# Matmul shapes and order in a hybrid attention step: prompt's values in four column tiles, new keys' scores over the whole array, sample's values in one stretch

## The chip, the cores and the metric

## What is computed

One layer of a decoder step, for a fresh prompt of 512 tokens and for 8 sequences with 8 new tokens each and a cache of 2048 positions. In short:

```python
proj = einsum('btd,de->bte', x, w_in)                     # D_MODEL 1024 -> 4096
q, k, v, g_att, gb, gc, hh, g_conv = split(proj, 8 x 512)
# attention, 8 heads of 64: keys at distance 0..128, 0..512 step 4, 0..2048 step 16;
# the branches are merged by their softmax denominators
att  = dilated_attention(q, k_all, v_all) * silu(g_att)
u    = gc * hh
z    = gb * conv3(u) * silu(g_conv)                       # depthwise, causal
out  = concat(att, z) @ w_out                             # 1024 -> 1024
y    = layer_norm(alpha * x + out)
# outputs: y of both groups, the new keys and values of the prompt, the shifted
# key and value caches of the samples (all 2048 positions), the last rows of u
```

The three branches read the same scores, so the kernel adds the logarithm of how many branches see a key to its score and does one softmax. Of the cache, 1280 of 2048 positions are read by a query ("used"); all of them are copied to the output.

## The kernel before

**Tokens and tiles.** There are 576 tokens (512 of the prompt, 64 of the samples), in two halves of 288 columns. A projection tile is 128 of the 4096 output features. `project(tile, h)` makes one half of one tile: 8 steps over the 1024 input features, each with three products of a split operand (high by high, low by high, high by low; lines 1137 to 1139), so 24 matmuls of 128x288 into bank `pj_a` (h = 0) or `pj_b` (h = 1). The weights of a tile come by a DMA into `w_raw`; ScalarE rounds them to `w_hi` (`split_hi`, L467) and VectorE makes the rest, `w_lo` (L773). Both hold two tiles.

**Rounds.** There are four rounds, one for each pair of heads. A round is written out by hand in `pe_round` (the first three) and `pe_last_round`, and the queues of the other engines (`act_round`, `dve_round`, the SP program of DMA issues) in the same manner. Every engine takes its own list in order; semaphores tie them. The eight tiles of a round that are projected are, in PE's order, C, H, B and the convolution's gate, the next round's values, the attention's gate, and the next round's queries and keys.

**Between the projections** stand small matmuls on plain float32. TensorE takes a float32 matmul in two passes, and the trace shows each pass as a record of its own (a transpose is one record). For the prompt there are, in three steps a round, scores (L1209), transposes of the probabilities (L1227) and values (`prompt_values`, L1241, output `po`). For the samples there are scores against the cached keys in four pieces (`sample_scores`, L1261, output `sc`, each sequence's queries in 32 columns of `q_bd`), scores against the 64 new keys (L1267), transposes (L1281, L1283), the products with the cached values in ten pieces (`sample_values`, L1297, again in `sc`) and with the new values (L1304).

A matmul whose stationary operand has 64 or 32 columns is placed by its output partitions on one of two or of four column strips of the array. `prompt_values` uses two strips of 64 columns (one for each head of the pair), `sample_scores` and `sample_values` four of 32.

**The order around the change.** In each of the first three rounds `prompt_values` of a step stands directly ahead of a piece of `sample_scores`. In the last round two of the three stand directly behind one. The end of a round is, in PE's order: project the attention gate's second half; `sample_turn(i, 2)`; `sample_values` 0 to 4; project the next queries; `sample_values` 5 to 9 with the new values; project the next keys.

**What sample_values waits for.** Piece t waits for its own load (`v_in`) and for the moves of the transposed probabilities from PSUM to `pt_s` by ScalarE: pieces 0 to 3 for the first move, 4 to 7 for the second, 8 for the third (L596) and 9 for the fourth (L597). ScalarE's list there is

```python
move_sample(i, 0)
move_sample(i, 1)
exp_gate(gate_tile(i), 1)
split_hi(t0 + 7)
move_sample(i, 2)      # the third and the fourth move
copy_q(i + 1)
```

so the last two moves stand behind the rounding of tile t0 + 7, the next round's keys: tile 10, 18 and 26 in the three rounds.

**DMA.** SP issues the loads of `w_raw`, `k_buf`, `v_buf` and `w_out` (queue q1), each when its buffer is free. ScalarE issues the copies of the caches from DRAM to DRAM (queue q10), spread over its list and not waited for until the end.

After the rounds the output projection runs over five tiles of tokens (L1454 to L1456). For the tile t = 1 it waits for `x_lo` (L927), which stands on VectorE behind the last splits of `w_out` (L915) and the last half of a gate.

Of the kernel before, what the change touches and what calls it, by code (L numbers as in the profile page):

```python
# [7 lines left out]
P = 128  # L8
D_MODEL = 1024
SEQ = 512  # L10
DEC_BATCH = 8
# [11 lines left out]
NS = DEC_BATCH * DEC_SEQ  # L23
NT = SEQ + NS
# [4 lines left out]
NPAIR = DEC_BATCH // 2  # L29
# [12 lines left out]
K_COLS = USED // K_PIECES  # L42
K_SLOT = DEC_BATCH * K_COLS
V_PIECES = 10
# [41 lines left out]
def layer_step(nc, d):  # L86

    with ExitStack() as ctx:
# [57 lines left out]
        sc = bank("sc")  # L146
# [109 lines left out]
        def unit_cols(u):  # L256

            c0 = width(2) if u == 3 else 0
            return c0, c0 + width(u)
# [6 lines left out]
        def qbd_copy_ap(e):  # L266

            a = q_bd[e * 64:e * 64 + 64, e * 8:e * 8 + 8]
            return bass.AP(tensor=a.tensor, offset=a.offset, ap=[[DEC_BATCH * 32, 64], [64, NPAIR], [48, 2], [1, 8]])

        def diagonal_ap(e):

# [859 lines left out]
        def _(pe):  # L1132
# [97 lines left out]
            def prompt_values(i, s):  # L1230

                pe.wait_ge(pr_moved, 2 * (N_STEPS * i + s) + 2)
                if s == 0 and i:
                    pe.wait_ge(pr_out, i)
                for u in STEPS[s]:
                    t = QT - 1 - u
                    for k in range(t + 1):
                        for e in range(2):
                            v = k * P + e * 64
                            c = e * SEQ + unit_cols(u)[0] + k * P  # L1240
                            last = nc.tensor.matmul(po[e * 64:e * 64 + 64, t * P:(t + 1) * P], v_rows[:, v:v + 64],  # L1241
                                                    pt_pr[:, c:c + P], start=(k == 0), stop=(k == t))
                last.then_inc(pr_pv, 1)

            def sample_scores(i, c):
                n = K_PIECES * i + c
                pe.wait_ge(k_in[c], 16 * (i + 1))
                if c == 0:
                    pe.wait_ge(qbd_done, 2 * (i + 1))
                    if i:  # L1250
                        pe.wait_ge(s_out, i)
                if n:
                    pe.wait_ge(s_masked, n)

                ends = c == K_PIECES - 1
                for b in range(2):
                    for r in range(NPAIR):
                        q = q_bd[:, (2 * r + b) * 32:(2 * r + b + 1) * 32]
                        k0 = c * K_SLOT + (2 * r + b) * K_COLS  # L1260
                        last = nc.tensor.matmul(sc[r * 32:r * 32 + 32, 0:K_COLS], q, k_buf[:, k0:k0 + K_COLS],  # L1261
                                                start=(b == 0), stop=(b == 1 and not ends), skip_group_check=True)
                if ends:
                    for b in range(2):
                        for r in range(NPAIR):
                            q = q_bd[:, (2 * r + b) * 32:(2 * r + b + 1) * 32]
                            last = nc.tensor.matmul(sc[r * 32:r * 32 + 32, K_COLS:K_COLS + NS], q,  # L1267
                                                    qk[:, NT + SEQ:],
                                                    start=False, stop=(b == 1), skip_group_check=True)
                last.then_inc(k_used, 1)  # L1270

            def sample_turn(i, g):
# [13 lines left out]
            def sample_values(i, t):  # L1286

                n = V_PIECES * i + t
                ends = t == V_PIECES - 1
                pe.wait_ge(s_moved, 4 * i + (t // 4 + 1 if not ends else 4))  # L1290
                if t == 0:
                    pe.wait_ge(s_masked, K_PIECES * (i + 1))
                pe.wait_ge(v_in[n % V_SLOTS], 16 * (n // V_SLOTS + 1))
                for b in range(2):
                    for r in range(NPAIR):
                        v0 = n % V_SLOTS * 1024 + (2 * r + b) * P
                        last = nc.tensor.matmul(sc[r * 32:r * 32 + 32, b * P:(b + 1) * P],  # L1297
                                                pt_s[:, t * P + r * 32:t * P + r * 32 + 32], v_buf[:, v0:v0 + P],
                                                start=(t == 0 and b == 0), stop=False, skip_group_check=True)
                last.then_inc(v_used, 1)  # L1300
                if ends:
                    for b in range(2):
                        for r in range(NPAIR):
                            last = nc.tensor.matmul(sc[r * 32:r * 32 + 32, b * P:(b + 1) * P],  # L1304
                                                    pt_s[0:NS, USED + r * 32:USED + r * 32 + 32],
                                                    v_new[:, i % 2 * P:(i % 2 + 1) * P], start=False, stop=True,
                                                    skip_group_check=True)
                    last.then_inc(s_pv, 1)
# [8 lines left out]
            def pe_round(i):  # L1317
                t0 = tile0(i)
                project(t0 + C, 0)
                if i:  # L1320
                    sample_out_turn(i - 1)
                prompt_scores(i, 0)
                project(t0 + C, 1)
                sample_scores(i, 0)
                project(t0 + H, 0)
                prompt_turn(i, 0)
                prompt_scores(i, 1)
                project(t0 + H, 1)
                prompt_values(i, 0)
                sample_scores(i, 1)  # L1330
                project(t0 + B, 0)
                prompt_turn(i, 1)
                prompt_scores(i, 2)
                pe.wait_ge(u_done, i + 1)
                project(t0 + B, 1)
                prompt_values(i, 1)
                sample_scores(i, 2)
                project(t0 + G_CONV, 0)
                prompt_turn(i, 2)
                pe.wait_ge(z_done, i + 1)  # L1340
                project(t0 + G_CONV, 1)
                prompt_values(i, 2)
                sample_scores(i, 3)
                project(v_tile(i + 1), 0)
                project(v_tile(i + 1), 1)
                project(gate_tile(i), 0)
                turn_v(i + 1)
                sample_turn(i, 0)
                sample_turn(i, 1)
                project(gate_tile(i), 1)  # L1350
                sample_turn(i, 2)
                for t in range(0, 5):
                    sample_values(i, t)
                project(q_tile(i + 1), 0)
                project(q_tile(i + 1), 1)
                for t in range(5, V_PIECES):
                    sample_values(i, t)
                project(k_tile(i + 1), 0)
                project(k_tile(i + 1), 1)

# [216 lines left out]
```

## Time and profile before

| what | us |
|---|---|
| median of 3 runs | 361.42 |
| the three runs | 361.47, 359.41, 361.42 |
| span of the profiled execution, first to last instruction | 356.6 |
| TensorE busy in it | 347.5 |
| VectorE, ScalarE, GpSimd busy | 201.2, 117.3, 10.6 |

The profile gives the span of the execution that it took, not that execution's device time. The span is 4.8 us below the median of the timed runs and 2.8 us below the lowest; what is left lies ahead of the first instruction and behind the last. In the chain of waits each piece has the time from the end of the piece before it to its own end, so the pieces of an engine that never waits add up to its span; a matmul's record by itself is longer than that, since matmuls overlap.

### The profile page before, as it was taken

Reading aid. Unit: us, or ns where it says so; the run is one execution under the profiler, and the core shown is the slowest. Engines: PE = TensorE matmul, PEld = TensorE weight load, DVE = VectorE, ACT = ScalarE, POOL = GpSimd, SP = SyncE. Lnnn points to the kernel's source line nnn. Section 1 sums busy time; section 2 is a strip of 40 time slices with the busy share of each in tenths; the row PEclk is TensorE's granted clock in tenths of the full one; section 3 lists DMA queues with packets and bytes.
Section 4 is the critical chain, followed back from the end, with each engine's and each line's share of the span. In section 5 each row is a group of like instructions: output and inputs, shape, how many; then the busy total and the mean of one; then the engine's idle time right before and its main releaser. Section 6 shows DMA issues by size and latency. Waiting matters only on the chain.

```text
span 356.6 us, 7735 instructions
## 1 busy us (share of the span) xinstructions
PE 347.5 (97%) x3290; PEld 312.2 (88%) x3290; DVE 201.2 (56%) x379; ACT 117.3 (33%) x231; POOL 10.6 (3%) x28
## 2 busy tenths in 40 slices
PE   7999999999999999999999999999999999999992
PEld 5998988899998888999988889999788998888782
DVE  4534438854134649561346573821456499877775
ACT  5523324342144233421332423412533635230000
POOL 0000000000100000001000000000000000300000
PEclk9999999999999999999999999999999999999998
DMA  8999999999999999999999999999999999999992
GB/s 299 403 422 414 417 417 417 418 421 420 418 396 418 417 416 381 369 422 385 411 408 415 421 414 420 427 421 419 421 412 413 415 417 371 399 364 347 361 364 112
DMA packets 34549, 141.06 MB, mean 396 GB/s; under 512 B 3410, under 2 KB 3794, under 8 KB 32466
## 3 DMA queue, kind: packets, MB, share of 16 engines
q1 hardware_dynamic: 18050, 73.20, 51.0%
q10 hardware_dynamic: 16464, 67.37, 47.9%
q8 instruction: 26, 0.43, 0.4%
q14 instruction: 9, 0.07, 0.0%
HBM read 135.80 MB, written 71.86 MB: 582 GB/s over the span
## 4 chain that ended last, share of the span: by engine, by line
PE 96%; DVE 1%; DMA 1%; DVEq 0%; ACT 0%; issue 0%
PE pj_a L1137 11%; PE pj_b L1137 10%; PE pj_b L1139 10%; PE pj_a L1138 10%; PE pj_b L1138 10%; PE pj_a L1139 10%; PE sc L1261 5%; PE sc L1297 5%; PE px L1209 3%; PE po L1241 3%; PE px L1454 3%; PE px L1456 3%; PE px L1455 3%; PE pt L1227 2%; PE pt L1281 1%; DMA k_buf<-in_first 1%
## 5 line engine op out<-in xcount | busy, mean ns | idle before, releaser
L1137 PE MATMUL pj_a<-x_hi,w_hi 128*128 128x288 f32 x256 | 78.1, 305 | 1.2 <-DVE x_lo L779 1.2
L1137 PE MATMUL pj_b<-x_hi,w_hi 128*128 128x288 f32 x256 | 77.5, 303 | 0.0
L1138 PE MATMUL pj_a<-x_lo,w_hi 128*128 128x288 f32 x256 | 75.5, 295 | 0.0
L1138 PE MATMUL pj_b<-x_lo,w_hi 128*128 128x288 f32 x256 | 75.5, 295 | 0.0
L1139 PE MATMUL pj_b<-x_hi,w_lo 128*128 128x288 f32 x256 | 75.4, 294 | 0.0
L1139 PE MATMUL pj_a<-x_hi,w_lo 128*128 128x288 f32 x256 | 75.3, 294 | 0.0
L1137 PEld LDWEIGHTS pj_a<-x_hi,w_hi 128*128 128x128 f32 x256 | 48.0, 187 | 8.5 <-issue 6.2
L467 ACT CAST w_hi<-w_raw 128x1024 fp32r<-128x1024 f32 x30 | 31.4, 1046 | 65.5 <-PE pj_b L1139 32.8
L773 DVE TENSOR_TENSOR w_lo<-w_raw,w_hi 128x1024 fp32r<-128x1024 f32 x30 | 36.7, 1223 | 28.7 <-ACT w_hi L467 28.7
L1137 PEld LDWEIGHTS pj_b<-x_hi,w_hi 128*128 128x128 f32 x256 | 48.0, 187 | 2.3 <-issue 1.3
L1139 PEld LDWEIGHTS pj_b<-x_hi,w_lo 128*128 128x128 f32 x256 | 48.2, 188 | 0.0
L1139 PEld LDWEIGHTS pj_a<-x_hi,w_lo 128*128 128x128 f32 x256 | 48.2, 188 | 0.0
L1138 PEld LDWEIGHTS pj_b<-x_lo,w_hi 128*128 128x128 f32 x256 | 48.1, 188 | 0.0
L1138 PEld LDWEIGHTS pj_a<-x_lo,w_hi 128*128 128x128 f32 x256 | 48.1, 188 | 0.0
L876 DVE RECIPROCAL rg<-rg 128x288 f32<-128x288 f32 x16 | 31.2, 1953 | 0.6
L838 DVE CUSTOM_DVE_ANT_0 p_pr<-px,mask_pr 128x512 f32<-128x512 f32 (+3 forms) x32 | 14.1, 488 | 16.9 <-PE px L1209 16.9
L566 ACT ACTIVATE p_pr<-p_pr,stat 128x512 f32<-128x512 f32 (+3 forms) x32 | 17.7, 553 | 13.6 <-DVE stat L838 13.6
L1261 PE MATMUL sc<-k_buf,q_bd 128*32 128x320 f32 x256 | 20.5, 439 | 0.0
L1297 PE MATMUL sc<-v_buf,pt_s 128*32 128x128 f32 x640 | 19.5, 274 | 0.0
L1297 PEld LDWEIGHTS sc<-v_buf,pt_s 128*32 128x32 f32 x640 | 16.9, 110 | 1.8 <-issue 1.8
L572 ACT COPY pt_pr<-pt 128x384 f32<-128x384 f32 (+1 forms) x24 | 11.2, 517 | 21.7 <-PE pt L1227 21.6
L1456 PE MATMUL px<-wo,x_lo 128*128 128x512 f32 (+1 forms) x40 | 14.8, 370 | 0.0
(153 smaller groups left out, 434.9 us busy)
## 6 DMA issues: line engine op xcount, KB each, us to landing
k_buf<-in_k_used SPq DMA_DIRECT2D x16, 1280.0 KB, 13.8
v_buf<-in_v_used SPq DMA_DIRECT2D x40, 512.0 KB, 19.0
out_k_used_out<-in_k_used ACTq DMA_DIRECT2D x16, 1280.0 KB, 17.2
out_v_used_out<-in_v_used ACTq DMA_DIRECT2D x20, 1024.0 KB, 16.9
w_raw<-in_w_tiles SPq DMA_DIRECT2D x30, 512.0 KB, 13.0
out_k_rest_out<-in_k_rest ACTq DMA_DIRECT2D x12, 1024.0 KB, 11.6
out_v_rest_out<-in_v_rest ACTq DMA_DIRECT2D x12, 1024.0 KB, 12.7
wo_raw<-in_w_out SPq DMA_DIRECT2D x8, 512.0 KB, 20.9
```

What stands on the lines that cost most here:

```text
L467: nc.scalar.copy(w_hi[:, c], w_raw[:, c]).then_inc(w_hi_done, 1)
L566: nc.scalar.activation(p, p, ACT.Exp, bias=negmax_pr[:, st:st + 1], scale=-1.0, accum_out=sum_pr[:, st:st + 1]).then_inc(pr_exp, 1)
L572: nc.scalar.copy(pt_pr[:, e * SEQ:e * SEQ + step_width(s)], pt[e][:, 0:step_width(s)])\
L773: nc.vector.tensor_tensor(w_lo[:, c], w_raw[:, c], w_hi[:, c].bitcast(F32), ALU.subtract)\
L838: nc.vector.tensor_tensor_reduce(out=p_pr[:, e * SEQ + c0:e * SEQ + c1], in0=px[e][:, c0:c1], in1=mask_pr[:, SEQ - width(u):], scale=-SCAL ...
L876: nc.vector.reciprocal(rg[:, c], rg[:, c]).then_inc(g_step, 1)
L1137: nc.tensor.matmul(out, w_hi[:, w], x_hi[:, c], start=(k == 0), stop=False)
L1138: nc.tensor.matmul(out, w_hi[:, w], x_lo[:, c], start=False, stop=False)
L1139: return nc.tensor.matmul(out, w_lo[:, w], x_hi[:, c], start=False, stop=(k == KT - 1))
L1261: last = nc.tensor.matmul(sc[r * 32:r * 32 + 32, 0:K_COLS], q, k_buf[:, k0:k0 + K_COLS], start=(b == 0), stop=(b == 1 and not ends), skip_ ...
L1297: last = nc.tensor.matmul(sc[r * 32:r * 32 + 32, b * P:(b + 1) * P], pt_s[:, t * P + r * 32:t * P + r * 32 + 32], v_buf[:, v0:v0 + P], sta ...
L1456: last = nc.tensor.matmul(out, m_lo, wo[:, hi], start=False, stop=(n == KT - 1))
```

## The change

Three edits, all in TensorE's list, and one access pattern for GpSimd that follows from the second.

1. `prompt_values` makes each product of 64 columns as two of 32. The matmuls double in number (from 80 to 160, from 160 records to 320) and use four column strips.
2. The scores against the new keys take the whole of a half of `q_bd` as one stationary operand of 128 columns. Per round 8 matmuls with 32 columns become 2 with 128; 64 moving columns each, as before. For this `q_bd` is laid out by half first, and GpSimd's copy into it writes with other strides.
3. In the first three rounds `sample_values` 0 to 9 stand in one stretch, ahead of the projection of the next queries. The last round keeps its order.

```diff
@@ qbd_copy_ap
-            return bass.AP(tensor=a.tensor, offset=a.offset, ap=[[DEC_BATCH * 32, 64], [64, NPAIR], [48, 2], [1, 8]])
+            return bass.AP(tensor=a.tensor, offset=a.offset, ap=[[DEC_BATCH * 32, 64], [32, NPAIR], [P + 16, 2], [1, 8]])
@@ prompt_values
-                        for e in range(2):
-                            v = k * P + e * 64
-                            c = e * SEQ + unit_cols(u)[0] + k * P
-                            last = nc.tensor.matmul(po[e * 64:e * 64 + 64, t * P:(t + 1) * P], v_rows[:, v:v + 64],
+                        for f in range(4):
+                            v = k * P + f * 32
+                            c = f // 2 * SEQ + unit_cols(u)[0] + k * P
+                            last = nc.tensor.matmul(po[f * 32:f * 32 + 32, t * P:(t + 1) * P], v_rows[:, v:v + 32],
                                                     pt_pr[:, c:c + P], start=(k == 0), stop=(k == t))
@@ sample_scores
-                        q = q_bd[:, (2 * r + b) * 32:(2 * r + b + 1) * 32]
+                        q = q_bd[:, b * P + r * 32:b * P + r * 32 + 32]
...
                 if ends:
                     for b in range(2):
-                        for r in range(NPAIR):
-                            q = q_bd[:, (2 * r + b) * 32:(2 * r + b + 1) * 32]
-                            last = nc.tensor.matmul(sc[r * 32:r * 32 + 32, K_COLS:K_COLS + NS], q,
-                                                    qk[:, NT + SEQ:],
-                                                    start=False, stop=(b == 1), skip_group_check=True)
+                        last = nc.tensor.matmul(sc[:, K_COLS:K_COLS + NS], q_bd[:, b * P:(b + 1) * P],
+                                                qk[:, NT + SEQ:],
+                                                start=False, stop=(b == 1), skip_group_check=True)
@@ pe_round
-                for t in range(0, 5):
+                for t in range(V_PIECES):
                     sample_values(i, t)
                 project(q_tile(i + 1), 0)
                 project(q_tile(i + 1), 1)
-                for t in range(5, V_PIECES):
-                    sample_values(i, t)
                 project(k_tile(i + 1), 0)
                 project(k_tile(i + 1), 1)
```

Where the second and first edits fall: TensorE, first round, the difference of the two kernels around the third step of the prompt's values and the last piece of the sample's scores (`po` is the prompt's output, `sc` the sample's bank, 32x320 means 32 stationary and 320 moving columns, x8 eight such matmuls in a row).

```order
 L1139 MATMUL pj_b<-x_hi,w_lo 128x288
-L1241 MATMUL po<-pt_pr,v_rows 64x128 x6
+L1241 MATMUL po<-pt_pr,v_rows 32x128 x12
 L1261 MATMUL sc<-k_buf,q_bd 32x320 x8
-L1267 MATMUL sc<-qk,q_bd 32x64 x8
+L1265 MATMUL sc<-qk,q_bd 128x64 x2
 L1137 MATMUL pj_a<-x_hi,w_hi 128x288
```

The prompt's values and the sample's scores now have the same form of tile, and the new keys' scores have the form of the projection behind them.

TensorE, end of the first round, before: the first stretch of the sample's values with what stands around it, and then (behind the dots) the second, with the 48 matmuls of the next queries' tile between them.

```order
L1281 MATMUL pt<-ident,p_s 128x128 x2
L1283 MATMUL pt<-ident,p_s 64x128
L1297 MATMUL sc<-v_buf,pt_s 32x128 x40
L1137 MATMUL pj_a<-x_hi,w_hi 128x288
...
L1139 MATMUL pj_b<-x_hi,w_lo 128x288
L1297 MATMUL sc<-v_buf,pt_s 32x128 x40
L1304 MATMUL sc<-v_new,pt_s 32x128 x8
L1137 MATMUL pj_a<-x_hi,w_hi 128x288
```

The same place in the changed kernel, whose lines 1279, 1281, 1295 and 1302 are 1281, 1283, 1297 and 1304 of before:

```order
L1279 MATMUL pt<-ident,p_s 128x128 x2
L1281 MATMUL pt<-ident,p_s 64x128
L1295 MATMUL sc<-v_buf,pt_s 32x128 x80
L1302 MATMUL sc<-v_new,pt_s 32x128 x8
L1137 MATMUL pj_a<-x_hi,w_hi 128x288
```

The second forty matmuls and the new values' eight moved ahead of the queries' tile. ScalarE's, VectorE's and SP's lists are the same in both kernels. 
## Rows read from the trace of the kernel before

**Rows 1.** The page: busy time by engine, granted clock, chain by engine.

```profile
PE 347.5 (97%) x3290; PEld 312.2 (88%) x3290; DVE 201.2 (56%) x379; ACT 117.3 (33%) x231; POOL 10.6 (3%) x28
PEclk9999999999999999999999999999999999999998
PE 96%; DVE 1%; DMA 1%; DVEq 0%; ACT 0%; issue 0%
```

**Rows 2.** Chain of waits, whole span: start, us, what. First and last round.

```profile
44.51 1.02 PE po L1241 x16
45.54 1.21 PE sc L1261 x16
...
55.05 0.81 PE po L1241 x12
...
257.22 1.03 PE po L1241 x16
```

**Rows 3.** Chain of waits, 63.8 to 67.2 us: around the new keys' scores.

```profile
65.09 1.22 PE sc L1261 x16
66.30 0.22 PE sc L1267 x16
66.52 0.33 PE pj_a L1137
66.86 0.13 PE pj_a L1138
```

**Rows 4.** Chain of waits, 75.9 to 94 us: transposes and the sample's values.

```profile
76.86 0.87 PE pt L1281 x8
77.73 0.13 PE pj_b L1137
...
81.25 2.32 PE sc L1297 x80
83.57 0.33 PE pj_a L1137
```

**Rows 5.** Chain of waits, whole span, last round: shorter stretches of the same.

```profile
282.66 1.01 PE sc L1297 x32
...
295.86 1.88 PE sc L1297 x64
```

**Rows 6.** Timeline of ScalarE, third round, with idle time before and its releaser.

```profile
226.48 0.41 ACT L584 ACTIVATE rg<-pj_b 128x288 f32<-128x288 f32 x1 [1.87 <-PE pj_b L1139]
230.28 1.05 ACT L467 CAST w_hi<-w_raw 128x1024 fp32r<-128x1024 f32 x1 [3.39 <-DMA w_raw<-in_w_tiles]
231.23 0.36 ACT L596 COPY pt_s<-pt 128x256 f32<-128x256 f32 x1
231.50 0.26 ACT L597 COPY pt_s<-pt 64x128 f32<-64x128 f32 x1
```

**Rows 7.** The same of ScalarE in the first round.

```profile
82.47 0.26 ACT L597 COPY pt_s<-pt 64x128 f32<-64x128 f32 x1
```

**Rows 8.** Timeline of TensorE, third round: where the sample's values begin.

```profile
226.70 0.75 PE L1297 MATMUL sc<-v_buf,pt_s 128*32 128x128 f32 x20
```

**Rows 9.** Timeline of SP: loads of values 8 and 9, tile 26, keys.

```profile
204.69 1.60 SPq L299 DMA_DIRECT2D v_buf<-in_v_used  x2
215.53 0.33 SPq L284 DMA_DIRECT2D w_raw<-in_w_tiles  x1
215.90 0.43 SPq L291 DMA_DIRECT2D k_buf<-in_k_used  x1
```

**Rows 10.** Landing of these loads: the two of values, then the keys' piece.

```profile
DMA to landing us min/median/max: 19.4/20.6/21.8
...
DMA to landing us min/median/max: 19.0/19.0/19.0
```

**Rows 11.** Landing of tile 18's load, issued at 142.8; then of all tiles.

```profile
DMA to landing us min/median/max: 3.8/3.8/3.8
...
DMA to landing us min/median/max: 3.8/13.0/21.1
```

**Rows 12.** Table by windows: busy us by engine, clock, DMA share, GB/s.

```profile
200.00:300.00 100.00, 100.00 (x1132) 90.18 (x1131) 58.57 (x111) 38.26 (x73) 1.05 (x5) 1.00 1.02 416
```

**Rows 13.** Timelines around the output projection's tile t = 1: ScalarE, VectorE, TensorE.

```profile
301.44 1.05 ACT L619 CAST wo<-wo_raw 128x1024 fp32r<-128x1024 f32 x1 [1.45 <-DMA wo_raw<-in_w_out]
...
307.89 2.51 DVE L927 TENSOR_TENSOR x_lo<-mix,x_hi 128x1024 fp32r<-128x1024 f32 x2
...
309.49 0.47 PE L1454 MATMUL pt<-wo,x_hi 128*128 128x512 f32 x1
```

## The prediction

> **What bounds the kernel now.** I read the page first: TensorE is busy 347.5 of 356.6 us, the granted clock is 9 tenths or more in all slices up to the last (the 2.4 GHz level), and the chain that ended last is 96% TensorE [rows 1]. The reader should see that no engine and no DMA makes TensorE wait; time is won or lost by what its own list takes, until a wait appears. The chain of waits was the second view, since its pieces run from end to end and so show what each stretch really takes [rows 2 to 5]. The third was who is nearly late: ScalarE's and SP's timelines ahead of the sample's values, because the third edit uses ScalarE's last two moves earlier [rows 6 to 11].
>
> **The price of a change of form.** Among the sample's values, 32 records take 1.01 us, 64 take 1.88 and 80 take 2.32 [rows 4, 5]. They go in groups of four strips, so 12 groups more cost 1.31 us: 0.109 us a group, and 1.01 - 8 x 0.109 = 0.14 us once, on entering four strips from the full array. Behind a stretch the first projection matmul takes 0.33 us in place of 0.13 [rows 3, 4]: leaving strips costs 0.20. Transposes with a full stationary operand are followed by 0.13 [rows 4], so there it costs nothing. Prompt's values in two strips: 16 records 1.02 us, 12 records 0.81 [rows 2], which at 0.109 a pair leaves 0.15 for entering. The sample's scores stand directly behind them and take 1.21 us for four groups of 320 columns [rows 2]. At 0.109 x 320 / 128 = 0.27 a group that is 1.09, so entering four strips from two costs 0.12 again.
>
> **Edit 1, prompt's values in four strips.** Twice the records, but four to a group in place of two: as many groups as before, 20 a round. The nearest row for a group of four with 128 moving columns is that of the sample's values, 0.109 us, the same as a pair costs now. So the products themselves change by 0 (if only two of four overlapped, see the rivals). What goes is one entry where the step touches a piece of sample scores: 0.15 + 0.12 before, 0.14 after, 0.13 to 0.15 saved, 0.14 taken. There are nine such places in the first three rounds and two in the last: 11 x 0.14 = 1.5 us, all on the path. The bound on the small side is 0, if the drain between the two comes from something other than the form.
>
> **Edit 2, new keys' scores over the whole array.** Before: 16 records in 0.22 us (four groups of 64 columns, 0.055 each) and 0.20 for leaving the strips behind them [rows 3]. After: the leaving comes ahead of them, and two matmuls in two passes make four records in a row, each with 128 stationary columns, and the projection follows at no extra cost. Nothing in the trace has 128 stationary and 64 moving columns in float32. From below such a record costs what streaming 64 columns does, 0.055 (then the four take 0.22 and the edit costs 0); from above what the nearest full record does, the transpose, 0.87 / 8 = 0.109 [rows 4] (then 0.44, and the edit costs 0.22). I take the upper one, because the transposes have the same stationary operand, 128 by 128 in float32, and loading it does not get shorter with the moving side: 0.21 a round, 0.85 us for four. A gain is excluded, since the same columns stream through at least as slowly as now.
>
> The Trainium skill, TensorE: Matmul & The Clock Gate, section LDWEIGHTS, says that a load of the stationary operand takes its columns divided by 1.2 GHz, whatever the rows; for 128 columns that gives 0.107 us. By it the four records take 0.43 us and the edit costs 0.21 a round; without such a floor it costs nothing. The trace's 0.109 for transposes agrees, but they also stream 128 columns, so that row does not decide. It speaks against this edit.
>
> **Edit 3, one stretch.** Of the first three rounds each loses one leaving (0.20) and one entry (0.14): 0.34, together 1.0 us. The 20 + 20 groups and the 48 projection matmuls only trade places. The sum on TensorE alone: -1.5 + 0.85 - 1.0 = -1.7 us. The queries' tile ends later by about 2.7 us, with the new keys' load, ScalarE's copy and rounding of the following tile behind it; the keys' tile (6.4 us, 48 x 0.133) covers that.
>
> **The wait that edit 3 adds.** Piece 8 of the values now starts 8 x 4 x 0.109 = 3.5 us after the first, and waits for ScalarE's third move; piece 9 for the fourth. Before, both had the queries' tile for cover. In the first round the last move starts at 82.47 and takes 0.26 [rows 7], against piece 8 at about 81.2 + 3.5 = 84.7: 2 us to spare. The second round runs alike. In the third ScalarE has the gate's exponential done at 226.9 and then sits idle 3.39 us for the load of tile 26; the rounding runs from 230.28, and the third move from 231.23 to 231.59 [rows 6]. Piece 0 starts at 226.70 [rows 8], so piece 8 would start at 230.2 on the old clock. TensorE gets there earlier: each of rounds one and two wins 3 x 0.14 + 0.34 - 0.21 = 0.55, the third until there 0.42 - 0.21 = 0.21, in sum 1.3, so it arrives at 228.9.
>
> How much earlier does tile 26 land? The two loads of values issued at 204.69 land 19.4 and 21.8 us later, near 224 and 227, tile 26, issued at 215.53, at 230.28, and the keys' piece behind it, at 215.90, 19.0 us later [rows 6, 9, 10]. They come one behind the other, at a DMA share of 1.00 [rows 12]. In such a queue an earlier issue of the one load moves nothing; the whole queue must run earlier. It was last short at 142.8, where tile 18's load took 3.8 us [rows 11], and there TensorE is ahead by 0.55 + 0.21 = 0.76. So I take 0.8, between 0 and 1.3. Then the third move ends at 231.6 - 0.8 = 230.8 and TensorE **waits 1.9 us** there. Queued behind the wait are the rest of the values, the queries' and keys' tiles and with them the whole next round. The last round then adds 2 x 0.14 - 0.21, a gain of 0.1. Sum: three rounds -1.65, wait +1.9, last round -0.1, so about +0.2 us: 356.6 becomes 356.8. With a shift of 1.3 it is -0.3, with none +1.0. The span lies 4.8 us below the median of the runs, and nothing ahead of the first instruction or behind the last is touched, so 361.4 becomes **361.6 us**.
>
> **Rivals.** *No wait.* If tile 26 lands by 227.6 (231.59 - 230.28 = 1.3 us ahead of 228.9), the wait is gone and the gain stays. For it: landings of tiles spread from 3.8 to 21.1 us [rows 11], a run without the profiler may have a freer queue, and no other tile makes trouble. Against: 2.7 us earlier than now. It would not keep all 1.7, though: tile t = 1 of the output projection starts at 309.49, while `x_lo` is ready at 307.89 + 2.51 / 2 = 309.15, behind a ScalarE split that waited for the last load of `w_out` until 301.44 [rows 13]. That leaves 0.34 plus the shift of the loads, 0.8: between -1.1 and -1.7, so 359.7 to 360.3.
>
> *Late landing, slower.* The same wait in the third round, with the load of tile 26 later than before by d, because the copies come in earlier and share the queues at a share of 1.00 [rows 12]: the change is +1.0 + d. It is slower than before from a landing at 229.3 on (old clock), and over 1% from d = 2.6, a landing near 232.9. With d of 0 to 1.5, 362.4 to 363.9.
>
> *The drain stays.* If the engine also empties between prompt's values and sample scores of one form, edit 1 wins nothing; TensorE then reaches piece 8 at 230.2, waits about 1.4 us, and the sum is -1.0 + 0.85 + 1.4, so 362.6. Against: no such gap shows within the 80 records in a row [rows 4].
>
> *Four do not overlap.* If pairs of prompt's values share something that two strips hide, 80 groups take 0.109 more each, +8.7 us, 370. Against: the sample's values do just this at 0.109.
>
> **How the numbers follow.** Forecast, a wait of about 2 us and a change of -0.3 to +1.0: 0.50. No wait: 0.28. Late landing with over +1.0: 0.13, of which 0.03 above 1%. Drain stays: 0.06. No overlap: 0.03. A measurement of this kernel, whose three runs spread 0.6%, can tell about 1%, 3.6 us. No case but the last and the end of the late one passes that upward; downward only the whole gain with a lucky base would, 0.05. So faster 0.05, same 0.89, slower 0.06. The range goes from 359.3 (no wait, with 0.4 for the scatter of the runs) to 363.3 (a landing 0.9 late).
>
> **What would show it.** In the changed profile: prompt's values near 1.0 and 0.8 us as before, the sample scores behind them 1.09 in place of 1.21 or the values shorter by as much; four records of new keys in about 0.44, with 0.13 for the projection matmul behind; one stretch of 160 records near 4.5 us; and in the third round a gap of 1 to 3 us ahead of piece 8, released by ScalarE's L596 behind a rounding that waited for a DMA. If the gap is missing, the no-wait rival holds; if it is over 3 us, the late one. The prediction is most easily wrong in the landing of one load.

## The result

| kernel | median | runs | range |
|---|---|---|---|
| before | 361.39 us | 20 | 358.72 to 363.90 |
| changed | 363.96 us | 20 | 361.74 to 367.44 |

The ratio is 1.0076, with a 95% interval of 1.0058 to 1.0093: the change makes the kernel slower by 2.7 us (2.1 to 3.4). The median lies outside the range of the forecast, 0.7 us above its upper end. It stays below the 1% that the forecast named as what such a measurement can tell, but 20 runs a side tell it clearly from none.

The profiled execution of the changed kernel has a span of 364.6 us and took 366.37 us, toward the upper end of its runs. These are the lines of its page that answer to [rows 1].

```profile
PE 350.0 (96%) x3402; PEld 316.2 (87%) x3402; DVE 200.8 (55%) x379; ACT 117.1 (32%) x231; POOL 10.9 (3%) x28
...
PEclk9999999999999999999999999989999999999998
...
PE 33%; DMA 10%; DVE 2%; ACT 1%; DVEq 0%; issue 0%
```

The chain now runs through a DMA, and one slice has a lower clock. The chain's shares add up to less than half of the span here, so the reading goes by another view. The view of waits on TensorE says who was waited for, how long in total, how often and the longest:

```profile
PE sc L1295 <- ACT pt_s L596: 3.4, 1, 3.4
PE sc L1302 <- issue: 1.8, 1, 1.8
...
PE sc L1295 <- issue: 0.5, 1, 0.5
```

The first is the wait that the forecast named. The other two are "issue": TensorE stood still and waited for nothing that the profile shows. In time they come first. TensorE's timeline in round one, then in round two, then in round three:

```profile
82.26 4.58 PE L1295 MATMUL sc<-v_buf,pt_s 128*32 128x128 f32 x160
86.76 0.63 PE L1302 MATMUL sc<-v_new,pt_s 64*32 64x128 f32 x14
89.22 0.40 PE L1302 MATMUL sc<-v_new,pt_s 64*32 64x128 f32 x2 [1.83 <-issue]
...
156.73 4.12 PE L1295 MATMUL sc<-v_buf,pt_s 128*32 128x128 f32 x138
161.34 0.85 PE L1295 MATMUL sc<-v_buf,pt_s 128*32 128x128 f32 x22 [0.49 <-issue]
...
229.95 3.70 PE L1295 MATMUL sc<-v_buf,pt_s 128*32 128x128 f32 x128
237.07 1.08 PE L1295 MATMUL sc<-v_buf,pt_s 128*32 128x128 f32 x32 [3.42 <-ACT pt_s L596]
```

In round three TensorE stops after 128 records, so ahead of piece 8, as forecast. In round one it stops between the 14th and the 15th of the 16 records of the new values, in round two after 138 records, in the middle of piece 8. No instruction there waits for a semaphore: only the first of a piece does. From the start of the record ahead of a stop to the start of the one behind it, the two stops are 2.1 and 0.8 us; the table below gives all stops in this way.

ScalarE around the wait of round three, the answer to [rows 6]:

```profile
229.76 0.46 ACT L584 ACTIVATE rg<-pj_b 128x288 f32<-128x288 f32 x1
235.70 1.04 ACT L467 CAST w_hi<-w_raw 128x1024 fp32r<-128x1024 f32 x1 [5.48 <-DMA w_raw<-in_w_tiles]
236.65 0.37 ACT L596 COPY pt_s<-pt 128x256 f32<-128x256 f32 x1
```

It stood idle 5.48 us for tile 26 where it was 3.39 before. Behind the wait the table by windows shows the clock (the number ahead of the DMA share); 0.50 is the 1.2 GHz level:

```profile
233.50:237.00 3.50, 0.15 (x8) 0.00 (x0) 2.08 (x4) 1.30 (x3) 0.00 (x0) 1.00 1.04 430
...
239.20:242.40 3.20, 3.20 (x15) 3.20 (x14) 0.00 (x0) 0.00 (x0) 0.00 (x0) 0.50 1.00 418
242.40:245.60 3.20, 3.20 (x25) 3.20 (x25) 0.00 (x0) 0.40 (x1) 0.00 (x0) 1.00 1.02 425
```

In the window at the lower clock 15 projection matmuls ran where 25 fit at full clock: the chain has 0.24 us for each in place of 0.13, about 1.5 us lost on top of the wait.

### The profile page after: what moved, and what is told of

It reads as the page before. It is cut to its first block and busy times, and to the rows that moved or that the text cites. A ratio compares the mean times of both kernels' runs of the same rounds, so it can differ in the third digit from the quotient of the medians.

```text
span 364.6 us, 7959 instructions
## 1 busy us (share of the span) xinstructions
PE 350.0 (96%) x3402; PEld 316.2 (87%) x3402; DVE 200.8 (55%) x379; ACT 117.1 (32%) x231; POOL 10.9 (3%) x28
## 5 line engine op out<-in xcount | busy, mean ns | idle before, releaser
L1137 PE MATMUL pj_a<-x_hi,w_hi 128*128 128x288 f32 x256 | 78.9, 308 | 0.9 <-DVE x_lo L779 0.9
L1138 PE MATMUL pj_a<-x_lo,w_hi 128*128 128x288 f32 x256 | 76.6, 299 | 0.0
L1139 PE MATMUL pj_a<-x_hi,w_lo 128*128 128x288 f32 x256 | 76.3, 298 | 0.0
L1137 PEld LDWEIGHTS pj_a<-x_hi,w_hi 128*128 128x128 f32 x256 | 49.1, 192 | 7.3 <-issue 5.7
L1138 PEld LDWEIGHTS pj_a<-x_lo,w_hi 128*128 128x128 f32 x256 | 49.2, 192 | 0.0
L1139 PEld LDWEIGHTS pj_a<-x_hi,w_lo 128*128 128x128 f32 x256 | 49.2, 192 | 0.0
L815 DVE COPY qk<-pj_b 128x288 f32<-128x288 f32 x4 | 1.8, 457 | 27.2 <-PE pj_b L1139 27.2
```

The costliest lines, as they stand in the source:

```text
L1137: nc.tensor.matmul(out, w_hi[:, w], x_hi[:, c], start=(k == 0), stop=False)
L1138: nc.tensor.matmul(out, w_hi[:, w], x_lo[:, c], start=False, stop=False)
L1139: return nc.tensor.matmul(out, w_lo[:, w], x_hi[:, c], start=False, stop=(k == KT - 1))
```

## Two places, six blocks apart

I numbered TensorE's records (weight loads, matmuls and its own semaphore instructions) in order of time. The stops of rounds one and two stand ahead of numbers 1729 and 3265. The difference is 1536, which is 6 x 256. Both are 193 beyond a multiple of 256.

DMA queue q8 carries packets of kind "instruction", 16 KB each, 27 in the changed kernel. I call a number that is 193 beyond a multiple of 256 a border, and what stands between two borders a block. In the changed kernel's trace the first 25 packets each start 0.3 to 4.6 us after TensorE passes a border, one for each; the last two, in the output projection, start 1.1 and 1.8 us ahead of theirs. In the trace without cache copies (below) 14 of the 27 start ahead of their border, by up to 3.9 us. The queues in two windows, as packets, MB and share of the 16 engines: first the 3.2 us after number 1473 is passed (83.5 us), then the 1.3 us behind them.

```profile
q1 hardware_dynamic: 118, 0.90, 67.0%
q10 hardware_dynamic: 117, 0.48, 36.5%
...
q1 hardware_dynamic: 31, 0.26, 46.7%
q10 hardware_dynamic: 69, 0.24, 46.2%
q8 instruction: 1, 0.02, 4.6%
```

This reads as if a block were asked for at the latest when the border one block ahead of it is passed. Here its packet got its turn 3.3 us later, beside loads and copies: it starts at 86.79 and ends at 87.75 us, and the block that it would bring begins at 89.22, 1.5 us behind the packet's end. That a packet brings just this block is inferred from such times; behind every stop named below, TensorE goes on 1.2 to 1.5 us after the end of its packet. Between borders TensorE has 256 instructions in hand. Among projection matmuls, one load and one matmul per 0.133 us, they last 17 us. In the stretch of the sample's values, four loads and four matmuls per 0.109 us, they last 3.5 us. So theory A: **TensorE runs dry where nearly a whole block of 256 instructions lies in a dense run**, because here a new block is there only 5.7 us after the border. The stretches of before, 160 and 192 loads and matmuls, were too short for that: the block that starts in the first of them took 8.8 us in each of the three rounds. The single one has 352, and 362 records with its semaphore instructions. Rival B: the extra instructions, or a long dense stretch as such, are slow wherever the borders lie.

The Trainium skill, Runtime: NRT & Kernel Launch, section Instruction fetch mechanics, describes the same blocks: 256 instructions, 16 KiB, fetched through a DMA queue of the sequencer's own while the current block runs. The trace agrees with that. The section also says that the fetch stays hidden because dispatch is slower than the fill; here it does not, by 2.1 us.

## The experiments

Each was timed against the kernel before, in turns on the same chip; the column in us is the ratio's distance from 1 times the 361.4 us of before.

| kernel | ratio (95%) | us | stops in the profile, rounds 1 / 2 / 3 |
|---|---|---|---|
| changed | 1.0076 (1.0058 to 1.0093) | +2.7 | 2.1 / 0.8 / 3.7 (wait) |
| values_four_strips | 0.9990 (0.9971 to 1.0009) | -0.4 | none |
| new_keys_full | 0.9985 (0.9954 to 1.0016) | -0.5 | none |
| values_and_keys | 0.9977 (0.9948 to 1.0006) | -0.8 | none |
| one_stretch | 1.0015 (0.9985 to 1.0046) | +0.5 | none / 0.3 / 2.2 (wait) |
| moves_first | 1.0058 (1.0034 to 1.0081) | +2.1 | 2.1 / 0.5 / none |
| phase_clear | 0.9999 (0.9970 to 1.0029) | 0.0 | none / none / 1.9 |
| phase_first | 1.0052 (1.0014 to 1.0090) | +1.9 | 2.2 / none / none |
| stretch_moves_first | 0.9996 (0.9973 to 1.0019) | -0.1 | none / none / 1.0 |
| stretch_shifted | 1.0144 (1.0104 to 1.0184) | +5.2 | 2.1 / 2.6 / 2.7 |
| strips_last_round | 1.0000 (0.9974 to 1.0025) | 0.0 | none / none / 0.8 |
| before_no_copies | 0.9923 (0.9891 to 0.9954) | -2.8 | none |
| after_no_copies | 0.9899 (0.9842 to 0.9956) | -3.6 | none |

### values_four_strips, new_keys_full, values_and_keys: edits 1 and 2 alone and together

Their edits are those of the change's diff, without the rest.

> Edit 1 alone on the kernel before. If entering four strips from two is what it saves, 11 x 0.14 = 1.5 us, it is 1.5 us faster (ratio 0.996), the sample scores behind a step take 1.09 in place of 1.21 us and the profile shows no wait on TensorE. If the drain between the two comes from something else, 0. If denser instructions alone were enough to starve TensorE, it would be slower, with a gap inside prompt's values.

> Edit 2 alone on the kernel before. With 0.109 us for each of the four records it costs 0.2 us a round, 0.8 us in all (ratio 1.002); with records as short as their 64 columns, 0. Edit 2 as the cause of the whole loss would show here as +2.6 us.

> Edits 1 and 2 without edit 3 (the values of the sample in two stretches, as before). On TensorE's list 11 x 0.15 saved and 4 x 0.2 paid, 0.8 us less; no dense run is longer than 192 instructions, so no gap by theory A. The median then moves by 0 to -0.8 us, and what the change loses is all with edit 3. If the extra instructions of edit 1 starve TensorE wherever they stand, it is slower.

The chain of waits of values_four_strips, first round; [rows 2] and [rows 3] had 0.81 and 1.21 or 1.22 in these places:

```profile
64.27 0.79 PE po L1241 x24
65.07 1.08 PE sc L1261 x16
66.14 0.22 PE sc L1267 x16
```

Twice the records take the same time, and the entry ahead of the scores is gone: 0.15 us a place. The new values are transposed (L1159) once at the start and once near the end of each round. From the first time to the second this kernel needs 55.69 us and before 56.15, so 0.46 less for three places. For new_keys_full it is 56.37: 0.22 more. Its timeline there:

```profile
64.98 1.28 PE L1261 MATMUL sc<-k_buf,q_bd 128*32 128x320 f32 x16
66.20 0.66 PE L1265 MATMUL sc<-qk,q_bd 128*128 128x64 f32 x4
66.66 0.38 PE L1137 MATMUL pj_a<-x_hi,w_hi 128*128 128x288 f32 x1
66.88 0.29 PE L1138 MATMUL pj_a<-x_lo,w_hi 128*128 128x288 f32 x1
```

Before, the same piece of scores to the second projection matmul took from 65.02 to 66.69, 1.67 us; now 64.98 to 66.88, 1.90. Four records with 128 stationary columns do cost what transposes cost. Both sizes were as forecast, and neither edit brings a stop in the first three rounds. The times move little: the intervals of all three take in no change. They leave out two forecasts of mine. values_four_strips was to be 1.5 us faster and without a wait; its interval is -1.0 to +0.3 us, and its profile has new waits of 1.3 us at the output (L927) and 1.1 us late in the last round (L892). new_keys_full was to be 0.8 us slower, and its interval is -1.7 to +0.6 us. The times of the list are right to 0.01 or 0.02 us a place, but what is gained on it does not arrive in the device time.

### one_stretch: edit 3 alone

> Edit 3 alone on the kernel before. Theory A, two causes that need edit 3: the wait for ScalarE's third move in the third round (2 to 4 us, and a fallen clock behind it where it is long), and a gap where TensorE's next block of 256 instructions has not come. In the changed kernel the first and second round's gaps stand at TensorE instructions 1729 and 3265, 6 x 256 apart. Without edit 1's extra instructions the long stretch begins about 80 instructions earlier in the first round, so that only one block border (1473) falls inside it, and the next comes in the projection: no gap in rounds one and two; only the wait in the third, so 1 to 3 us slower. Rival B, a long dense stretch always starves TensorE: gaps of 0.5 to 2 us in rounds one and two as well.

Theory A held in the main: no stop in round one, and in round two only 0.3 us from start to start where 0.13 is usual, at number 3265, again a border. The stretches begin so that a border falls 157, 140 and 123 instructions in, and the rest of the next block runs at the projections' pace. In round three the wait for the third move was there, 1.88 us, without a lower clock behind it:

```profile
227.90 3.70 PE L1297 MATMUL sc<-v_buf,pt_s 128*32 128x128 f32 x128
233.48 0.75 PE L1297 MATMUL sc<-v_buf,pt_s 128*32 128x128 f32 x20 [1.88 <-ACT pt_s L596]
```

Yet the time is only 0.5 us above before, where I had put 1 to 3, and its interval (-0.5 to +1.7) takes in no change. So the wait does not carry the whole loss. From the second transposing of new values to the third, with round one's stretch between, the kernel needs 72.44 us and before 72.76: the two changes of form saved, 0.32.

### moves_first: the changed kernel without the wait of round three

```diff
                 exp_gate(gate_tile(i), 1)
-                split_hi(t0 + 7)
                 move_sample(i, 2)
+                split_hi(t0 + 7)
```

> The changed kernel, and ScalarE makes the third and fourth moves ahead of rounding tile t0 + 7. Theory: the wait of the third round goes with its clock drop, the two gaps of rounds one and two stay (1.8 and 0.5 us in the profile), since they wait for no semaphore. Then -1.7 + 2.3 = about +0.6 us against the kernel before. If the gaps are the echo of ScalarE's late moves, they go as well: -1.7 us.

```profile
85.42 0.63 PE L1302 MATMUL sc<-v_new,pt_s 64*32 64x128 f32 x14
87.88 0.40 PE L1302 MATMUL sc<-v_new,pt_s 64*32 64x128 f32 x2 [1.82 <-issue]
...
228.26 4.57 PE L1295 MATMUL sc<-v_buf,pt_s 128*32 128x128 f32 x160
```

The wait is gone, and the stops of rounds one and two stand at the same records as before. The ratio is 1.0058: most of the loss stays. I had put it at +0.6 us and it is +2.1 (1.2 to 2.9). The list's gain of 1.7 us does not arrive; the runs without copies point to the reason (below).

### phase_clear and phase_first: the same work with the borders moved

```diff
-            for _ in range(5):
+            for _ in range(3):
                 nc.tensor.matmul(sc[:, 0:256], rg[:, 0:P], rg[:, P:384], start=True, stop=True)
+            for _ in range(28):
+                nc.tensor.matmul(sc[0:32, 0:32], rg[:, 0:32], rg[:, P:P + 32], start=True, stop=True)
```

This is phase_clear, on top of moves_first; phase_first has 4 and 11 in place of 3 and 28, and 64 columns. These matmuls warm the engine at the start, where it waits for its first data.

> The kernel moves_first, with 104 more TensorE instructions ahead of everything: the warming matmuls at the start, on data that nothing reads, are 3 of 256 columns and 28 small ones instead of 5 of 256. Theory A, a gap appears where a whole block of 256 instructions lies in the dense stretch of 352: the shift puts the borders 253 instructions into the first round's stretch, 180 into the second's and 107 into the third's, one each with none following inside, so no gap in any round, and about 2.3 us less than moves_first. Rival B, a dense stretch of that length always starves, or the gap belongs to the 87th instruction of the new values: both gaps stay.

> The same with a shift of 40 instructions (4 warming matmuls of 256 columns and 11 small ones). Borders fall 61 and 317 instructions into the first round's stretch, 244 into the second's, 171 into the third's. Theory A: one gap of about 2 us, in the first round alone, 20 records earlier than before (at the 158th of the 176 records), none in the second. Rival B: both gaps, in the places they had.

In phase_first the stop of round one came 20 records earlier, after 154 of them, and that of round two was gone, with the same instructions in both stretches:

```profile
80.88 4.55 PE L1297 MATMUL sc<-v_buf,pt_s 128*32 128x128 f32 x154
87.37 0.42 PE L1297 MATMUL sc<-v_buf,pt_s 128*32 128x128 f32 x6 [1.93 <-issue]
...
156.98 4.58 PE L1297 MATMUL sc<-v_buf,pt_s 128*32 128x128 f32 x160
161.49 0.64 PE L1304 MATMUL sc<-v_new,pt_s 64*32 64x128 f32 x16
162.06 0.40 PE L1137 MATMUL pj_a<-x_hi,w_hi 128*128 128x288 f32 x1
```

In phase_clear both stops were gone, and 104 instructions more at the start made the kernel 2.1 us faster than moves_first (each against before). My expectation of no stop in any round failed: one came in round three, right behind the stretch.

```profile
229.83 0.64 PE L1304 MATMUL sc<-v_new,pt_s 64*32 64x128 f32 x16
232.07 0.29 PE L1137 MATMUL pj_a<-x_hi,w_hi 128*128 128x288 f32 x1 [1.59 <-issue]
```

It stands at number 5057, again a border: 255 of the block's 256 records lie in the stretch. The condition is not that a second border lies inside the stretch, but how fast the whole block is used up.

That is only half of it. In round one of phase_clear 253 of a block's 256 records lie in the stretch, and in round two of phase_first 244. I had left these two blocks out, and by theory A as it stood both should have starved TensorE. They were used up in 3.6 and 4.1 us, yet no stop came, because their packets started only 0.4 and 0.5 us after the border. With copies this delay goes by where the border lies. Here it was 0.4 and 0.5 us for a border just ahead of the stretch, 1.8 to 2.1 us for one 28 records in (the changed kernel, moves_first and values_and_keys in round two), and 2.7 to 4.0 us for one 61 to 171 records in. So a stop needs both: a block that is used up fast, and a border far enough inside the fast part for its packet to start late. The shift at the start decides both. A request that leads TensorE by some tens of instructions would explain the steps, since these last much longer among the projections; no run tests that.

### stretch_moves_first, stretch_shifted, strips_last_round: edit 3 with good and with bad borders

All three make ScalarE's moves first. stretch_shifted adds to edit 3 nothing but warming matmuls (4 of 256 columns and 16 of 32, so 60 instructions); strips_last_round adds edit 1 in the last round.

> Edit 3 alone on the kernel before, and ScalarE makes the third and fourth moves ahead of rounding tile t0 + 7. Borders of TensorE's blocks of 256 instructions fall 157, 140 and 123 instructions into the three stretches, as in one_stretch, which had no gap. Theory A: no gap and no wait in any round, 1.0 us less on TensorE's list; the median gains less, 0.3 to 1.0 us, since the output projection then waits for its last loads. Rival B (a long stretch starves by itself): gaps.

> The kernel stretch_moves_first with 60 more TensorE instructions at the start (4 warming matmuls of 256 columns and 16 small ones, on data that nothing reads). Borders fall 97, 80 and 63 instructions into the three stretches and again 353, 336 and 319 in, so that nearly all of a block of 256 lies in the dense part. Theory A: a gap of 0.5 to 2.2 us near the end of each of the three stretches, 1.5 to 5 us slower than stretch_moves_first. If only edits 1 and 2 bring gaps, none.

> The kernel stretch_moves_first with edit 1 in the last round alone, where it moves no border of the three stretches: 0.3 us less on TensorE's list, no gap. It is the version that I expect to be the fastest, 0.3 to 1.2 us below the kernel before, near the bound of what the DMA engines let through.

stretch_shifted is the sharpest test: 60 instructions that stand where the engine waits for its first data cost 5.3 us against its twin, by the ratios of the two to before. Its three stretches, first to third round:

```profile
88.36 0.41 PE L1306 MATMUL sc<-v_new,pt_s 64*32 64x128 f32 x4 [1.83 <-issue]
...
164.82 0.65 PE L1306 MATMUL sc<-v_new,pt_s 64*32 64x128 f32 x8 [2.33 <-issue]
...
242.51 0.42 PE L1299 MATMUL sc<-v_buf,pt_s 128*32 128x128 f32 x5 [2.41 <-issue]
```

A stop in each, at numbers 1729, 3265 and 4801, and a lower clock behind each. The second is followed by 0.50 from 164.3 to 171.1 us, where 35 records ran in 6.8 us:

```profile
164.30:171.10 6.80, 6.28 (x35) 5.86 (x35) 0.00 (x0) 0.00 (x0) 0.00 (x0) 0.50 1.05 401
```

The profiled execution took 372.71 us, the longest of the six runs, so its stops may be longer than the typical ones; the 5.3 us between the twins are a little over the 5 that I had as the most. stretch_moves_first, expected without any stop, has one of 1.0 us in round three at number 4801, 17 records behind the stretch; 239 of its block's 256 lie in the stretch. I had put it 0.3 to 1.0 us below before, and it is 0.1 (-1.0 to +0.7). From passing one border to the first instruction behind the next, the stopped blocks took 4.1 to 6.2 us in all these traces: 5.7 and 4.3 in the changed kernel, 5.4 in phase_clear, 5.6 in stretch_moves_first, 5.7 to 6.2 in stretch_shifted.

strips_last_round was to be the fastest. Its median is 360.60 against 360.92 of before, ratio 1.0000: no version measured here is faster than before beyond doubt.

### before_no_copies and after_no_copies: the queue emptied

```diff
+                return
                 n = next(copies)
...
-            sp.wait_ge(copied, 16 * (2 * REST_ROWS + NPAIR * (K_PIECES + V_PIECES // 2)))
```

> The changed kernel without the copies of the two caches from DRAM to DRAM (the new caches are not written apart from the new rows). If the gaps are blocks of instructions that come late because the DMA engines are full, they shrink to under 0.5 us, and the wait for the third move goes, since tile 26 lands early. If the fetch has a fixed delay, the gaps of 2.1 and 0.8 us stay. Against before_no_copies it should be 1.5 to 1.8 us faster where no gap is left: the sum on TensorE alone.

> The kernel before without these copies (left out in the same manner), as the reference for after_no_copies. It has no wait to lose, so its span stays near 356 us less what the end costs.

Both stops and the wait went. The stretch of round one, the same 352 instructions over the same borders:

```profile
82.31 4.57 PE L1295 MATMUL sc<-v_buf,pt_s 128*32 128x128 f32 x160
86.81 0.64 PE L1302 MATMUL sc<-v_new,pt_s 64*32 64x128 f32 x16
87.38 0.40 PE L1137 MATMUL pj_a<-x_hi,w_hi 128*128 128x288 f32 x1
```

The block asked for at 83.55 us now starts to move 0.5 us later and has landed at 85.0, ahead of the border at 87.07. From the first transposing of new values to the last transposing of the samples' output (L1312 in the one, L1314 in the other), after_no_copies needs 287.9 us and before_no_copies 289.5: 1.6 us less, the sum on TensorE alone as forecast. The medians are 357.28 us (four runs) and 358.49 us (ten runs). So the change is a gain on the list where the DMA engines have room, and by these few runs in the time too: 1.2 us.

They also show that the copies cost the kernel before 2.8 us, though its profile had no wait behind the start. Where is not shown for that kernel, since its one profile has none; the profile of values_and_keys, a run of 361.83 us, suggests the places: late in the last round and at the output.

```profile
PE pj_b L1137 <- DVE mix L892: 0.8, 1, 0.8
PE px L1452 <- DVE wo L915: 0.7, 1, 0.7
PE pt L1452 <- DVE x_lo L927: 0.4, 1, 0.4
```

moves_first, stretch_moves_first and strips_last_round have the same three waits. They stand behind loads: in values_and_keys ScalarE sits idle 4.95 us for a load of `w_out` there, and 2.75 in the profile before. So what TensorE gains earlier it can lose there.

## Why the prediction was wrong

**Edit 1** was right in mechanism and size: 0.14 us a place forecast, 0.15 measured, no cost for twice the records.

**Edit 2** was right: 0.21 us a round forecast, 0.22 measured. The upper of the two bounds was the true one.

**Edit 3, its gain** was right: 0.34 a round forecast, 0.32 measured. The sum of the three, -1.7 us, came out at -1.6 on the list without the copies.

**The step that failed** is the sentence on edit 3 that the groups and the projection matmuls "only trade places". They do in time on the array, but not in instructions a microsecond. Putting the two stretches together made a dense run of 352, longer than a block, and TensorE ran dry twice, 2.9 us in the profile. None of the rivals had this. The rival of a late landing reaches to within 0.1 us of the measured time, 363.9 against 363.96 us, but by the wait in round three alone; moves_first has no such wait and is still 2.1 us slower than before, so that closeness is luck. The cause is shown by phase_first, phase_clear and stretch_shifted, which move the stops, take them away or make three of them by instructions ahead of everything, and by after_no_copies, where the blocks come in time. That the 16 KB packets are these blocks is read from their times and their number. Which of the borders are bad follows from how many instructions stand ahead, so edit 1 had a part: alone harmless, it adds 80 instructions a round and moved the borders from where edit 3 alone has almost no stop (one_stretch) to where it has two.

**The wait for the third move** was right in place and cause, and mis-sized: 1.9 us forecast, 1.9 in one_stretch, 3.4 in the changed kernel's profile with 1.5 us more for the clock, which the forecast left out. In the timed runs it weighs less: without it the kernel goes from +2.7 to +2.1 us, and the two intervals overlap, so its part is 0 to 2 us and not settled closer.

**The landing of the loads.** I let the queue run 0.8 us earlier with TensorE. In the profile tile 26 landed at 235.70, 5.4 us later than before. Its load was issued 4.4 us later (219.95 in place of 215.53) and took 1.0 us more to land. Of the 4.4 us, 3.2 are TensorE's delay by then (tile 24's projection starts at 221.63 in place of 218.47), and 1.3 of these stem from the start of the program; the rest is not explained further.

**The base.** The forecast took the 4.8 us between the profiled span and the median for time outside the first and last instruction. In every run on record that time is 1.7 to 1.9 us, so the profiled execution itself took about 358.4 us, 3 us less than the median and less than the lowest of the 20 runs. "No engine and no DMA makes TensorE wait" [rows 1] was true of it and, it seems, not of the typical execution. I took its lack of waits for the kernel's. Its span is 0.1 us above that of before_no_copies, 356.6 against 356.5, while the two kernels differ by 2.8 us in the timed runs. The cap in the rival without a wait, at tile t = 1 of the output, was the right mechanism: TensorE waits for L927 in eight of the profiles here.

## What to carry to other kernels

Small matmuls packed into column strips use up instructions faster than large ones, here at 4.9 times the pace (eight in 0.109 us against two in 0.133). Where the DMA engines are full, as here, look at how many of them stand in a row: stretches of 160 and 192 cost nothing here, 352 cost 2 to 5 us where the borders fell badly. Large matmuls between two stretches, as before the change, are a remedy. A gap named "issue" in the middle of a run, at numbers that differ by a multiple of 256, points to this. Before counting a gain on the busiest engine, ask whether the profile shown is a typical execution: here 0.8 us less on TensorE's list (values_and_keys) moved the time by 0.8 and 1.6 us less (values_four_strips) by 0.4, both within the scatter, and the profiles of both show waits behind the last loads that the one before does not.

## What the runs showed that I had not expected

- A block of 256 TensorE instructions is asked for at the latest when the border ahead of it by one block is passed. With DMA share near 1.00 it came 4.1 to 6.2 us after the border where TensorE stopped, and in time for 3.6 and 4.1 us in two other places; without the copies it came in time for 3.5 and 3.4 us.
- A stop of 1.9 us (phase_clear) or 2.2 us (phase_first) was followed by a stretch at the 1.2 GHz level, and one of 2.1 us in the changed kernel and in moves_first was not; behind one of 2.1 us in stretch_shifted the level fell as well.
- Float32 records with 128 stationary and 64 moving columns take as long as with 128 moving, 0.11 us.
- Two strips of 64 columns and four of 32 are different forms: going from one to the other costs 0.15 us though the array is never used whole in between.
